# An SSD scan in which the features' decay sums are not spread a second time: ScalarE reads them from the key banks before the mask is added

## The reference

```python
ac = a.reshape(b, nc, SSD_CHUNK, SSD_GROUPS, SSD_HEADS_PER_GROUP).transpose(0, 1, 3, 4, 2)
a_cum = jnp.cumsum(ac, axis=-1)
seg = a_cum[..., :, None] - a_cum[..., None, :]
decay_in = jnp.exp(jnp.where(causal, seg, -jnp.inf))
scores = jnp.einsum('bclgn,bcsgn->bcgls', cc, bc)
y_diag = jnp.einsum('bcgls,bcgels,bcsgep->bclgep', scores, decay_in, xc)
...
y_off = jnp.einsum('bclgn,cbgepn,bcgel->bclgep', cc, prev, jnp.exp(a_cum))
return (y_diag + y_off).reshape(b, l, h, p).astype(xdt.dtype)
```

## Time and profile before

| | us |
|---|---|
| median of 3 runs | 1629.5 |
| lowest, highest | 1629.44, 1630.66 |
| profiled execution, its own time | 1630.62 |
| its span, first to last instruction | 1628.8 |
| PE busy | 1609.4 (99%) |
| DVE busy | 1042.0 (64%) |
| ACT busy | 742.2 (46%) |
| POOL busy | 657.6 (40%) |

### The profile page before, as it was taken

The page is one execution under the profiler, slowest core; times in us unless marked ns, Lnnn a source line. Parts: engine busy times, 40 slices in busy tenths (PEclk is TensorE's granted clock), DMA queues, the critical chain, the costliest instruction groups (busy, mean ns, idle before and its releaser), DMA issues.

```text
span 1628.8 us, 22387 instructions
## 1 busy us (share of the span) xinstructions
PE 1609.4 (99%) x7908; PEld 1273.9 (78%) x7927; DVE 1042.0 (64%) x1662; ACT 742.2 (46%) x1287; POOL 657.6 (40%) x307
## 2 busy tenths in 40 slices
PE   7999999999999999999999999999999999999999
PEld 6688777777888888777788877777688888888887
DVE  6699686677346877767775177777676765565100
ACT  5423465565255655555543244444534444443210
POOL 4344653232544344344454332122244344444442
PEclk9999999999999999999999999999999999999999
DMA  6243221223333243211123221121233233233331
GB/s 211 79 117 103 79 85 59 65 63 132 95 112 91 65 158 119 65 52 53 52 78 91 80 77 52 53 66 52 91 111 91 78 106 100 91 102 93 101 95 60
DMA packets 40370, 143.40 MB, mean 88 GB/s; under 512 B 4500, under 2 KB 5172, under 8 KB 39900
## 3 DMA queue, kind: packets, MB, share of 16 engines
q1 hardware_dynamic: 37600, 131.96, 26.3%
q10 hardware_dynamic: 2684, 10.27, 1.9%
HBM read 137.63 MB, written 4.58 MB: 87 GB/s over the span
## 4 chain that ended last, share of the span: by engine, by line
PE 84%; issue 9%; DVE 3%; POOL 2%; ACT 1%; DMA 0%; POOLq 0%; SPq 0%; DVEq 0%; ACTq 0%
PE bank L791 18%; PE bank L793 18%; PE bank L792 18%; PE bank L1448 4%; PE bank L1447 4%; PE bank L1446 4%; PE bank L1332 2%; POOL w_lo L651 2%; PE bank L842 1%; PE bank L844 1%; PE bank L843 1%; PE bank L1353 1%; PE bank L1341 1%; PE bank L1235 1%; PE bank L1241 1%
## 5 line engine op out<-in xcount | busy, mean ns | idle before, releaser
L651 POOL TENSOR_TENSOR w_lo<-w_raw,w_hi 128x1024 fp32r<-128x1024 f32 x241 | 589.8, 2450 | 935.2 <-ACT w_hi L1476 797.9
L791 PE MATMUL bank<-u_hi,w_hi 128*128 128x512 f32 x768 | 327.0, 426 | 1.4 <-ACT gm L2031 0.8
L1476 ACT ACTIVATE w_hi<-w_raw 128x1024 fp32r<-128x1024 f32 x197 | 207.3, 1056 | 209.9 <-PE bank L793 169.3
L793 PE MATMUL bank<-u_hi,w_lo 128*128 128x512 f32 x768 | 302.4, 394 | 0.0
L792 PE MATMUL bank<-u_lo,w_hi 128*128 128x512 f32 x768 | 301.9, 393 | 0.0
L791 PEld LDWEIGHTS bank<-u_hi,w_hi 128*128 128x128 f32 x768 | 145.4, 189 | 42.6 <-issue 10.8
L793 PEld LDWEIGHTS bank<-u_hi,w_lo 128*128 128x128 f32 x768 | 145.5, 189 | 32.1
L792 PEld LDWEIGHTS bank<-u_lo,w_hi 128*128 128x128 f32 x768 | 145.9, 190 | 31.1 <-issue 3.2
L1446 PE MATMUL bank<-u_hi,w_hi 128*128 128x512 f32 x288 | 112.0, 389 | 0.0
L1447 PE MATMUL bank<-u_lo,w_hi 128*128 128x512 f32 x288 | 112.0, 389 | 0.0
L1448 PE MATMUL bank<-u_hi,w_lo 128*128 128x512 f32 x288 | 112.0, 389 | 0.0
(11 more groups left out here) (480 smaller groups left out, 3422.6 us busy)
## 6 DMA issues: line engine op xcount, KB each, us to landing
w_raw<-weights SPq DMA_DIRECT2D x243, 512.0 KB, 3.5
xt<-x_t SPq DMA_DIRECT2D x8, 256.0 KB, 6.4
hank<-bias_dram ACTq DMA_DIRECT2D x8, 256.0 KB, 4.1
xt<-x_t ACTq DMA_DIRECT2D x1, 2048.0 KB, 8.8
h_dram<-h_res ACTq DMA_DIRECT2D x1, 2048.0 KB, 7.7
h_res<-h_dram ACTq DMA_DIRECT2D x1, 2048.0 KB, 7.5
out<-h_res SPq DMA_DIRECT2D x8, 256.0 KB
p_val<-p_t ACTq DMA_DIRECT2D x1, 512.0 KB, 11.0
```

The source lines that it names most:

```text
L651: pool.tensor_tensor(w_lo[:, j, :], w_raw[:, j, :], w_hi[:, j, :].bitcast(F32), ALU.subtract).then_inc(w_lo_ready, 1)
L791: pe.matmul(o, hi, xh, start=(i == 0), stop=False)
L793: mm = pe.matmul(o, lo, xh, start=False, stop=(i == n - 1))
L1476: act.activation(w_hi[:, c % RING, :], w_raw[:, c % RING, :], ACT.Copy).then_inc(w_hi_ready, 1)
```

## The change

The second spreading of the sums is gone, and with it `spread_features`, the semaphore `e_spread` and the use of bank 2 in the scan. `spread_keys(p)` writes only the sums into banks 4 and 5, unmasked. `start_decays(p)` now takes its factors from there: the first 64 partitions from the one bank, the last 64 from the other, columns 128 to 511 (the first chunk has no entering state), two activations and no longer one. The new `mask_keys(p)` waits for them (`e_ready`, now counted twice a block), adds the mask to both banks, and counts `a_masked`, for which `key_decays(p)` waits.

In the order on PE `mask_keys(p+1)` stands behind `off_dot` of block p. On ACT `start_decays(p+1)` moves ahead of `after(t)`, so that the rounding of the weight chunk comes behind it, and `start_decays(0)` into the convolution stage, one tile ahead of `key_decays(0)`, which itself comes one tile later. A last wait before the kva tile, which uses bank 2 again, is now for `l_ready`.

```diff
@@ -1099,23 +1099,17 @@
 
                 if p:
                     pe.wait_ge(l_ready, 2 * p)
-                for s in range(2):
-                    pe.matmul(bank[4 + s][:, :], ident_b[:, :], later4_b[:, :], start=True, stop=False)
                 for h in (2 * p, 2 * p + 1):
                     k = slice(32 * (h % 4), 32 * (h % 4) + 3)
-                    pe.matmul(bank[4 + h % 2][:, :], ones_b[k, :], a_rows[k, h // 4, :], start=False,
+                    pe.matmul(bank[4 + h % 2][:, :], ones_b[k, :], a_rows[k, h // 4, :], start=True,
                               stop=True).then_inc(a_spread, 1)
 
-            def spread_features(p):
-
-                if p:
-                    pe.wait_ge(e_ready, p)
-                else:
-                    pe.wait_ge(dve_freed, [t for t in st["ssd_x"] if t["bank"] == 2][-1]["freed"][1])
-                for h in (2 * p, 2 * p + 1):
-                    r, k = slice(64 * (h % 2), 64 * (h % 2) + 64), slice(32 * (h % 4), 32 * (h % 4) + 3)
-                    mm = pe.matmul(bank[2][r, :], ones_b[k, 0:SSD_P], a_rows[k, h // 4, :], start=True, stop=True)
-                mm.then_inc(e_spread, 1)
+            def mask_keys(p):
+
+                for s in range(2):
+                    pe.wait_ge(e_ready, 2 * p + s + 1)
+                    pe.matmul(bank[4 + s][:, :], ident_b[:, :], later4_b[:, :], start=False, stop=True,
+                              skip_group_check=True).then_inc(a_masked, 1)
 
             def group_dot(g):
 
@@ -1171,8 +1165,10 @@
             spread_keys(0)
             pe.wait_ge(conv_ready, 2 * SSD_G)
             group_dot(0)
-            for t in st["ssd_x"][early:]:
+            for i, t in enumerate(st["ssd_x"][early:]):
                 column_tile(t, of_u2)
+                if i == 1:
+                    mask_keys(0)
             for g in range(SSD_G):
                 z = st["z"][4 * g]
                 if g:
@@ -1197,7 +1193,6 @@
                     pe.wait_ge(grp_copied, 2)
                     turn_x(g, 1)
                     column_tile(z, of_u2, part=(0, 5))
-                    spread_features(0)
                     column_tile(st["z"][1], of_u2, part=(0, 2))
                     pe.wait_ge(dve_freed, [t for t in st["ssd_x"] if t["bank"] == 3][-1]["freed"][1])
                     turn_x(g, 2)
@@ -1209,7 +1204,6 @@
                 if g:
                     chunk_state(g, 2)
                 spread_keys(4 * g + 1)
-                spread_features(4 * g + 1)
                 if not g:
                     chunk_state(g, 2)
                 column_tile(z, of_u2, part=(6, 8))
@@ -1226,7 +1220,6 @@
                             spread_group(g - 1)
                         if p + 1 < 16:
                             spread_keys(p + 1)
-                            spread_features(p + 1)
                         pe.wait_ge(y_read, p)
                     pe.wait_ge(w_ready, 2 * p + 2)
                     for c in range(NT):
@@ -1241,12 +1234,14 @@
                         mm = pe.matmul(bank[7][:, c * P:(c + 1) * P], states[:, c - 1, q * P:(q + 1) * P],
                                        c_t[:, g, c * P:(c + 1) * P], start=True, stop=True)
                     mm.then_inc(off_dot, 1)
+                    if p + 1 < 16:
+                        mask_keys(p + 1)
             column_tile(st["qa"][0], of_u2)
             column_tile(st["qa"][1], of_u2, part=(0, 4))
             group_sum(SSD_G - 1)
             column_tile(st["qa"][1], of_u2, part=(4, 8))
             spread_group(SSD_G - 1)
-            pe.wait_ge(e_ready, 16)
+            pe.wait_ge(l_ready, 32)
             column_tile(st["kva"][0], of_u2)
             def of_y(k):
                 return y_hi[:, k, :], y_lo[:, k, :]
@@ -1843,7 +1838,7 @@
             def key_decays(p):
 
                 for h in (2 * p, 2 * p + 1):
-                    act.wait_ge(a_spread, h + 1)
+                    act.wait_ge(a_masked, h + 1)
                     if h >= 4:
                         act.wait_ge(y_dot, h - 3)
                     for c in range(NT):
@@ -1853,10 +1848,12 @@
 
             def start_decays(p):
 
-                act.wait_ge(e_spread, p + 1)
                 if p >= 2:
                     act.wait_ge(y_ready, p - 1)
-                act.activation(e_ac[:, p % 2, :], bank[2][:, :], ACT.Exp).then_inc(e_ready, 1)
+                for h in (2 * p, 2 * p + 1):
+                    r = slice(64 * (h % 2), 64 * (h % 2) + 64)
+                    act.wait_ge(a_spread, h + 1)
+                    act.activation(e_ac[r, p % 2, P:S], bank[4 + h % 2][r, P:S], ACT.Exp).then_inc(e_ready, 1)
 
             def group_out(g):
 
@@ -1916,6 +1913,8 @@
 
                     act.wait_ge(cols_ready, 2)
                     group_out(0)
+                    start_decays(0)
+                if i == len(conv_tiles) - 3:
                     key_decays(0)
 
             def group_std(g):
@@ -1927,7 +1926,6 @@
                 act.activation(std_y[:, :], bank[3][:, 0:NT], ACT.Sqrt, bias=vec("eps"),
                                scale=1.0 / (4 * 4 * P)).then_inc(std_ready, 1)
 
-            start_decays(0)
             for g in range(SSD_G):
                 if g:
                     act.wait_ge(y_dot, 8 * g)
@@ -1947,10 +1945,11 @@
                     if p:
                         act.wait_ge(y_ready, p)
                     act.activation(z_sg[:, :], bank[t["bank"]][:, :], ACT.Tanh, scale=0.5).then_inc(z_ready, 1)
+                    if p + 1 < 16:
+                        start_decays(p + 1)
                     after(t)
                     if p + 1 < 16:
                         key_decays(p + 1)
-                        start_decays(p + 1)
                     if g and p % 4 == 0:
                         group_std(g - 1)
             act.wait_ge(y_ready, 16)
@@ -2732,7 +2731,7 @@
                     dve.wait_ge(y_dot, 2 * p + 2)
                     link(dve.scalar_tensor_tensor(yp, yp, vec("d_skip", p), bank[6][:, :], ALU.mult, ALU.add))
                     dve.wait_ge(off_dot, p + 1)
-                    dve.wait_ge(e_ready, p + 1)
+                    dve.wait_ge(e_ready, 2 * p + 2)
                     dve.tensor_tensor(e, bank[7][:, P:S], e, ALU.mult).then_inc(y_read, 1)
                     dve.wait_ge(y_read, p + 1)
                     link(dve.tensor_tensor(yp[:, P:S], yp[:, P:S], e, ALU.add))
```

More of the change, by code:

```diff
@@ L565, in build @@
         w_ready = sem("w_ready")
-        e_spread = sem("e_spread")
+        a_masked = sem("a_masked")
         e_ready = sem("e_ready")
```

## The result

The changed kernel takes 1637.0 us (median of 7, 1634.0 to 1637.5) against 1629.5 us (median of 7, 1626.0 to 1632.4): 0.41% slower, ratio 1.0041, 95% interval 1.0028 to 1.0054. In a second set of runs it was 1634.5 against 1629.0, ratio 1.0034 (1.0021 to 1.0047). I had forecast 1631.6, in a range up to 1634.6.

What follows compares the result with a forecast made beforehand. TensorE, busy 99%, was taken as the bound; 5.3 us of removed matmuls would become 7.4 us more waiting. Start 0.20, cycles 1.05 and end 0.85 sum to +2.1 us: 1631.6 from 1629.5, 80% range 1625.8 to 1634.6.

Steps and rivals of the forecast that it cites:

- The features' pair: TensorE, each block: the removed pair of matmuls costs 0.33 us; sixteen pairs make 5.3 us less.
- The masks move behind `off_dot`: TensorE: 0.46 us a block moves behind `off_dot`; masks come at T+1.92 (T: start of tanh) and wait 0 us.
- The product could start at T+0.21: TensorE: unless held, the product starts 0.79 us earlier, 0.20 us after the start of tanh (T) instead of 0.99.
- `y += e` is held by w_lo: VectorE, block 2 of a group: ready 2.84 us after tanh's start, held because GpSimd's w_lo started at 2.48.
- `weighted` ends at W+4.98: VectorE's chain behind the end of w_lo (W) stays the same; `weighted` for block 3 ends at W+5.00.
- The waits at blocks 3, 7 and 11: TensorE: a new wait for `weighted` of 1.67 us each; the group cycle grows 0.35 us, three cycles 1.05.
- The clock falls in the new waits: Rival, TensorE: five waits let the clock fall, some 1.6 us each, 8 us on top, 1639.6 us; chance 0.04.
- The pair of exps: ScalarE: two exps in place of one take 0.43 us each, 0.86 together, bounds 0.75 to 1.3.
- the load of 1.28 us: ScalarE, conv stage: the earlier `start_decays(0)` brings two more function-set loads of 1.28 us; cost 0, bound 0.5.
- slip ahead of w_lo: Rival: `y += e`, 0.36 us behind w_lo's start, goes first; -3.2 to -3.4 us, 1626.2 us; chance 0.14.
- The array's changes: Rival, TensorE: masks' new place costs two changes a block, 0.10 us each, +2.0 on top, 1633.6 us; chance 0.17.
- The full gain: Rival: the removed matmuls count in full because GpSimd does not hold VectorE; -5.3 us, 1624.2 us; chance 0.05.

Runs made afterwards that it cites:

- b4: Kernel before without the features' matmuls (factors all one) and with GpSimd's squares held until `weighted` of block 3 is done: 1624.3 us, ratio 0.9965.
- b1: Kernel before with GpSimd's squares of a group held until `weighted` of its block 3 is done: 1629.0 us, ratio 1.0004.
- a1: Changed kernel with GpSimd's squares of a group held until `weighted` of its block 3 is done: 1624.2 us, ratio 0.9980 to the kernel before.
- b3: Kernel before with the exp of the entering states moved ahead of the weight chunk's rounding, nothing else: 1633.1 us, ratio 1.0029.
- b2: Kernel before without the features' matmuls, factors of the entering states all one, squares not held: 1625.2 us, ratio 0.9981.
- a2: Changed kernel with ScalarE's rounding of the weight chunk put back ahead of the two exps: 1628.4 us, ratio 0.9999 to the kernel before.
- a4: Changed kernel with squares held until `weighted` of block 3 and the function set loaded by a tiny exp before the scan: 1624.4 us, ratio 0.9973.

## Why the prediction was wrong

**What held.** The features' pair is worth 0.33 us (b4 against b1: 4.3 for thirteen). The masks move behind `off_dot` and wait for nothing after block 0. The product could start at T+0.21 (forecast 0.20). `y += e` is held by w_lo, what follows it by the squares, and `weighted` ends at W+4.98 (forecast 5.00). The waits at blocks 3, 7 and 11 are new, 1.78 us (forecast 1.67), and that at block 15 grew to 2.11 (forecast 2.1). So the kernel became slower although 5.3 us of matmuls left TensorE's queue, and by the path that was forecast: a1 and b3 show it.

**The step that failed is the price of the new waits.** The sum counted them as idle time alone and the clock with nothing; "The clock falls in the new waits" was a rival at 0.04, left outside the range. Measured, two of the waits at blocks 3, 7, 11 and 15 were followed by a fall in one profiled execution and three in the other, at 1.6 us each (1.64 in the first). The rival's 1.6 us a fall was right, its chance was not, and its count of five falls was too high. The evidence against it was one idle of 1.40 us at the start of the kernel. But the profile before already had a row with half-clock time in it and no long idle, which I had not read:

```profile
1000.00:1040.00 40.00, 39.89 (x244) 30.34 (x243) 31.82 (x82) 18.86 (x46) 10.22 (x5) 0.96 0.21 67
```

With PE listed as busy for 39.89 of 40 us the granted clock was 0.96 there, and the mean clock of the span was 0.995. The two falls in the scan of the profiled execution, 3.3 us, are half of its 6.6; behind the scan it has five, as many as the one before.

**Two terms were mis-sized.** The pair of exps holds ACT for 1.00 us (731.79 to 732.79) and not 0.86: each 64x384 exp lasts 0.48 us and the next instruction starts 0.50 us after it, not 0.1 us before its end. So w_lo starts at T+2.64, not T+2.48, and the product of block 3 at T+10.17 of block 2, not T+10.01: 0.16 us in each of four groups, 0.6 us. And in block 0 the load of 1.28 us, which I had placed in the convolution stage only, held exps, rounding and masks. The masks, forecast to wait for nothing here too, waited 1.1 us, and tanh of block 2 came 15.64 us after that of block 0, forecast 15.30. That this is only 0.3 us more hides a second miss: `y += e` of block 0 was not held by w_lo, as the forecast had it, and the wait at the product of block 1 was 1.1 us and not 2.1. The first tanh was 0.15 us later than forecast; what held it is not shown. Together this is 1.1 us. Without falls the product of block 15 stands at 823.6, forecast 822.6. So the 6.6 us are 2.1 forecast, 1.0 for these terms, 3.3 for the clock and 0.2 behind the scan.

**The other rivals.** `y += e` did not slip ahead of w_lo; the longer exps had brought them to 0.22 us of each other, forecast 0.36. The array's changes cost nothing that shows: from the first matmul of `off_dot` to the second z matmul are 1.43 us with the masks (742.48 to 743.91), 0.43 more than the 1.00 before (738.99 to 739.99), and the masks' own time was read as 0.46. The full gain was worked out as impossible while POOL holds DVE, and b2 and b4 show it: 2.9 us of D with the squares where they were, 5.2 with the squares held back.

Left open: why a wait of the same length lets the clock fall at one block and not at another. The places change from run to run. In the scans of all twelve profiled executions there are sixteen waits of PE of 1.78 us or more, and eight were followed by a fall; a2 and a4 had one such wait each (2.05 and 1.97 us) and no fall. Of ten waits of 1.06 to 1.29 us one was, that in b3.

## What to carry to other kernels

An instruction put ahead of another on an idle engine costs nothing there, and still decides when a third engine starts, and so whom that one will hold; follow a moved rounding, copy or split to the operation that reads it, and see in the trace whom that one makes longer. Work taken from the bounding engine comes back only once the next product's other input is early enough: here, in the changed kernel, one wait on POOL's queue took 10.6 us from D, more than the 5.3 us of removed matmuls. Before a new wait of 1 to 2 us on TensorE is priced, look at the granted clock in narrow stretches of the whole trace. Where the wait cannot be avoided, matmuls to an unused bank can be cheaper than silence.

## What the runs showed of the hardware

TensorE fell to the half clock, as from 699.0 to 702.5 us and at a cost of 1.64 us, behind eight of sixteen waits of 1.78 to 2.11 us between dense stretches, and behind one of 1.29. With seven 0.23 us matmuls in each long wait it stayed at the full clock in the scan of the profiled execution. In the latent attention it fell two to five times in every profiled kernel, five times in the one before; in that kernel PE is listed as busy there for 39.2 to 39.9 us of each 40 (1000 to 1160 us). These falls make most of the scatter of the times (spans of the kernel before: 1624.1, 1625.6, 1627.2, 1628.8, 1630.2, with mean clocks from 0.998 down to 0.994).

A VectorE addition of 128x384 values with both inputs in SBUF takes 0.56 us alone, and 2.59 us where it starts 0.22 us behind a GpSimd subtraction of 2.40 us.

An ACT exp of 64 partitions and 384 columns from PSUM takes 0.48 us, as long as a copy of 128x384 (0.49), and the next instruction starts 0.50 us after it. Behind a 128x512 tanh of 0.60 us the next one starts after 0.50 us too (731.29, 731.79), so here the smaller activation freed the engine no earlier. An exp of 128x384 was not run.

Tanh needed no load behind sigmoid, exp did. The load lasted 1.28 us and the exp began 0.01 us after it.
